# Output projection of a conv and attention layer: one accumulated sum with normalised inputs, or two sums with the norm's factor applied at eviction

## The reference

```
y_attn = rmsnorm(y_attn, g_attn_out) * silu(z_attn)      # 512 channels
y_conv = rmsnorm(y_conv, g_conv_out) * silu(z_conv)      # 512 channels
y = concatenate([y_attn, y_conv], axis=-1) @ w_out       # (512, 1024) @ (1024, 1024)
x = x + gate[:, None, :] * y
return rmsnorm(x, g_final)                               # mean of squares per token, eps 1e-6
```

## Time and profile before

| | us |
|---|---|
| median of 3 runs (lowest, highest) | 285.13 (285.1, 285.28) |
| the profiled execution, its own time | 284.59 |
| its span in the profile | 282.8 |
| TensorE busy | 268.6 (95%) |
| VectorE busy | 197.0 (70%) |
| ScalarE busy | 141.1 (50%) |
| GpSimd busy | 115.0 (41%) |

### The profile page before, as it was taken

How to read it: one execution, slowest core, us unless ns; L and a number is a source line. 1 busy time by engine, 2 the same in 40 slices (tenths; PEclk the granted TensorE clock), 3 DMA queues, 4 the chain that set the end, 5 groups by cost and what they waited for, 6 DMA issues and landing times.

```text
span 282.8 us, 3727 instructions
## 1 busy us (share of the span) xinstructions
PE 268.6 (95%) x1292; PEld 222.1 (79%) x1292; DVE 197.0 (70%) x351; ACT 141.1 (50%) x237; POOL 115.0 (41%) x73
## 2 busy tenths in 40 slices
PE   5889999899999999999999999999999999999990
PEld 1567888688888888888888888888888878888880
DVE  4898888799989976889899865922773531305564
ACT  4845355367059733673633364637196583402331
POOL 2500001466433433191363322343356999922410
PEclk9999999999999999999999999999999999999998
DMA  5999944296702462067334102332503444500113
GB/s 204 381 417 419 406 186 129 72 418 203 255 3 74 122 194 96 0 233 288 112 82 141 52 27 74 111 72 96 206 14 137 153 145 167 206 0 2 75 74 149
DMA packets 12405, 43.82 MB, mean 155 GB/s; under 512 B 2145, under 2 KB 2145, under 8 KB 10978
## 3 DMA queue, kind: packets, MB, share of 16 engines
q1 hardware_dynamic: 12242, 43.32, 43.0%
q10 hardware_dynamic: 144, 0.26, 0.2%
HBM read 38.33 MB, written 2.10 MB: 143 GB/s over the span
## 4 chain that ended last, share of the span: by engine, by line
PE 74%; ACT 6%; issue 6%; POOL 4%; DVE 4%; DMA 3%; SPq 1%; POOLq 0%; ACTq 0%; DVEq 0%
PE ps L1009 17%; PE ps L1011 17%; PE ps L1010 17%; PE ps L1068 4%; POOL w_lo L579 3%; PE ps L1153 3%; PE ps L1083 2%; PE ps L1145 2%; DMA xt<-in_x 2%; PE ps L1089 2%; DVE mod_junk L688 2%; PE ps L1081 1%; PE ps L1087 1%; PE ps L1128 1%; PE ps L1127 1%
## 5 line engine op out<-in xcount | busy, mean ns | idle before, releaser
L579 POOL TENSOR_TENSOR w_lo<-raw,w_hi 128x1024 fp32r<-128x1024 f32 x29 | 74.1, 2559 | 123.8 <-ACT w_hi L327 123.7
L1009 PE MATMUL ps<-h_lo,w_hi 128*128 128x512 f32 x200 | 78.9, 395 | 0.0
L1011 PE MATMUL ps<-h_hi,w_hi 128*128 128x512 f32 x200 | 78.0, 390 | 0.0
L1010 PE MATMUL ps<-h_hi,w_lo 128*128 128x512 f32 x200 | 77.9, 389 | 0.0
L1011 PEld LDWEIGHTS ps<-h_hi,w_hi 128*128 128x128 f32 x200 | 37.6, 188 | 8.0
L1010 PEld LDWEIGHTS ps<-h_hi,w_lo 128*128 128x128 f32 x200 | 37.6, 188 | 7.2
L1009 PEld LDWEIGHTS ps<-h_lo,w_hi 128*128 128x128 f32 x200 | 37.6, 188 | 7.1
L688 DVE CUSTOM_DVE_ANT_0 mod_junk<-ada,c_bc 128x1024 f32<-128x1024 f32 x22 | 34.1, 1549 | 1.1
L327 ACT ACTIVATE w_hi<-raw 128x1024 fp32r<-128x1024 f32 x29 | 30.4, 1051 | 6.9 <-DMA raw<-in_wslots 6.9
L394 ACT ACTIVATE probs<-probs,rmin 128x384 f32<-128x384 f32 (+3 forms) x32 | 17.6, 552 | 30.0 <-DVE rmin L814 30.0
L824 DVE TENSOR_SCALAR probs<-probs,prec 128x384 f32<-128x384 f32 (+3 forms) x32 | 21.4, 733 | 0.3
(11 more groups left out here) (153 smaller groups left out, 503.3 us busy)
## 6 DMA issues: line engine op xcount, KB each, us to landing
raw<-in_wslots SPq DMA_DIRECT2D x33, 512.0 KB, 3.4
ada<-in_ada SPq DMA_DIRECT2D x11, 1024.0 KB, 8.9
raw<-in_whead SPq DMA_DIRECT2D x8, 448.0 KB, 7.2
xt<-in_x SPq DMA_DIRECT2D x4, 512.0 KB, 4.9
x<-in_x SPq DMA_DIRECT2D x4, 512.0 KB, 5.8
out<-x SPq DMA_DIRECT2D x3, 512.0 KB, 2.7
ada<-in_ada SPq DMA_DIRECT2D x2, 512.0 KB, 8.0
qs<-q_lo SPq DMA_DIRECT2D x16, 64.0 KB, 2.0
```

Source lines behind the costliest of these rows:

```text
L579: nc.gpsimd.tensor_tensor(lo, src[:, :], hi.bitcast(F32), ALU.subtract).then_inc(s_lo, 1)
L1009: nc.tensor.matmul(o, a_hi, b_lo, start=start, stop=False)
L1010: nc.tensor.matmul(o, a_lo, b_hi, start=False, stop=False)
L1011: return nc.tensor.matmul(o, a_hi, b_hi, start=False, stop=stop)
```

## The change

The factor is a number per token, and the projection's output has tokens on partitions. So y goes into the projection without it, and it is applied to the output. Since the halves have different factors, they can't share a sum.

- `y_diag`, `y_rows` and `y_scaled` are gone, for both halves.
- The conv half has a list of its own, `CONV`: pieces 0 to 6 and one of 512 columns in place of pieces 7 and 8. Both halves open and close their own sums in the same banks; the attention share of a piece starts once the conv share has been read (`om_ok`).
- VectorE evicts 17 times in place of 9, each with one scalar_tensor_tensor (bank × factor × gate) and the addition to x2: eight for conv, then nine for attention.
- The split of y no longer waits for the norm. `y_high(0, 0)` to `(0, 2)` and `y_low(0, 0)` to `(0, 2)` move up among the weight slots; for the attention half `y_high(1, ·)` waits for `attn_gated` and stands, as before, behind slot 32.
- `y_sums(1)` on VectorE moves from behind `join_halves(3, 1)` to behind the eviction of conv piece 1. `y_rstd(1)` stays where it is on GpSimd, between slots 29 and 30.

```
+    CONV = PIECES[:7] + [(3, 512, 1024, 3)]
+    NC = len(CONV)
...
-            def y_diag(g):
-                act.wait_ge(rs_ok, g + 1)
-                for m in range(TT):
-                    ins = nc.scalar.activation(diag[:, m, :], ident[:, :], ACT.Copy, scale=rsy[:, g, m:m + 1])
-                ins.then_inc(diag_ok, 1)
+            def y_high(g, p):
+                if g == 0:
+                    act.wait_ge(yc_gated, p + 1)
+                    act.wait_ge(mod_step, 2 * NADA)
+                else:
+                    act.wait_ge(ya_gated, p + 1)
+                    act.wait_ge(pv_out, 2 * NP)
+                nc.scalar.activation(group(g)[1][:, p], group(g)[0][:, p], ACT.Copy).then_inc(y_hi, 1)
...
-            def y_scaled(g, p):
-                dve.wait_ge(bc_out, g + 1)
-                dve.wait_ge((yc_gated, ya_gated)[g], p + 1)
-                y = group(g)[0][:, p]
-                nc.vector.tensor_tensor(y, y, bank((4, 3)[g]), ALU.mult).then_inc(y_norm, 1)
...
             join_halves(3, 1)
-            y_sums(1)
             attn_gated(3)
-            for p in range(NP):
-                y_scaled(1, p)
...
+            def residual(g, e):
+                m, lo, hi, b = (CONV, PIECES)[g][e]
+                i = NC * g + e
+                dve.wait_ge(acc_out[g], e + 1)
+                if i == 0:
+                    dve.wait_ge(gate_ok, 2)
+                if g == 0 and e % 2 == 0:
+                    dve.wait_ge(x2_in[m], 16)
                 if e == 0:
+                    dve.wait_ge(rs_ok, g + 1)
+                if i >= 2:
+                    dve.wait_ge(x2_ok, i - 1)
+                o = om[:, i % 2, 0:hi - lo]
+                nc.vector.scalar_tensor_tensor(out=o, in0=bank(b, 0, hi - lo), scalar=rsy[:, g, m:m + 1],
+                                               in1=gate[:, lo:hi], op0=ALU.mult, op1=ALU.mult).then_inc(om_ok, 1)
+                dve.wait_ge(om_ok, i + 1)
...
                 nc.vector.tensor_tensor(x2[:, m, lo:hi], x2[:, m, lo:hi], o, ALU.add).then_inc(x2_ok, 1)
+
+            for e in range(NC):
+                residual(0, e)
+                if e == 1:
+                    y_sums(1)
...
-            pe.wait_ge(y_norm, NP)
+            pe.wait_ge(ssq_ok, 1)
             project(0, 3)
-            y_rows(1)
...
             project(0, 6)
+            pe.wait_ge(ssq_ok, 2)
+            project(0, 7)
+            pe.wait_ge(om_ok, 2)
             for p in range(NP):
...
+                project(1, 0, [p])
+                project(1, 1, [p])
+            for e in range(2, len(PIECES)):
+                pe.wait_ge(om_ok, e + 1)
+                project(1, e)
```

More of the change, by code:

```diff
@@ L188, in build @@
         sq_add = [sem("sqc_add"), sem("sqa_add")]
[L189 to L191 removed]
+        ssq_out, ssq_ok, rs_ok = sem("ssq_out"), sem("ssq_ok"), sem("rs_ok")
+        y_hi, y_lo = sem("y_hi"), sem("y_lo")
         gcol_ok, gdiag_ok, gate_bc, gate_ok = sem("gcol_ok"), sem("gdiag_ok"), sem("gate_bc"), sem("gate_ok")
[L193 removed]
+        acc_out, om_ok, x2_ok, x2_sq, x2_g = [sem("acc_conv"), sem("acc_attn")], sem("om_ok"), sem("x2_ok"), sem("x2_sq"), sem("x2_g")
         last_sq, x2_left = sem("last_sq"), sem("x2_left")
@@ L496, in _ @@
             slot(20)
+            y_high(0, 0)
             other_half(2, 1)
@@ L500, in _ @@
             slot(21)
+            y_high(0, 1)
             exponents(3, 0)
@@ L505, in _ @@
             slot(23)
+            y_high(0, 2)
             square_y(0, 3)
@@ L517, in _ @@
             probs_high(3, 1)
-            y_high(0)
+            y_high(0, 3)
             silu("ZA3")
@@ L523, in _ @@
             slot(W_ATTN0 + 1)
-            y_diag(1)
             slot(W_ATTN0 + 2)
             slot(W_ATTN0 + 3)
-            y_high(1)
+            for p in range(NP):
+                y_high(1, p)
             def square_out(e):
                 m, lo, hi, _ = PIECES[e]
-                act.wait_ge(x2_ok, e + 1)
+                act.wait_ge(x2_ok, NC + e + 1)
                 if e:
@@ L589, in y_rstd, with y_low @@
                 nc.gpsimd.tensor_tensor(rsy[:, g, :], ssy[:, g, :], nhalf[:, 0:TT], ALU.pow).then_inc(rs_ok, 1)
[L591 to L596, removed]
+            def y_low(g, p):
+                pool.wait_ge(y_hi, NP * g + p + 1)
+                raw_y, hi, lo = group(g)
+                nc.gpsimd.tensor_tensor(lo[:, p], raw_y[:, p], hi[:, p].bitcast(F32), ALU.subtract).then_inc(y_lo, 1)
             for n in range(12):
@@ L612, in _ @@
             add_square(1, 2)
-            for n in range(21, 24):
-                slot(n)
+            y_low(0, 0)
+            slot(21)
+            y_low(0, 1)
+            slot(22)
+            slot(23)
+            y_low(0, 2)
             add_square(0, 3)
@@ L621, in _ @@
             slot(28)
-            y_low(0)
+            y_low(0, 3)
             add_square(1, 3)
@@ L627, in _ @@
                 slot(n)
-            y_low(1)
+            for p in range(NP):
+                y_low(1, p)
             for m in range(TT):
@@ L940, in _ @@
             attn_gated(2)
-            for p in range(NP):
-                y_scaled(0, p)
             join_halves(3, 0)
@@ L945, in _ @@
             join_halves(3, 1)
-            y_sums(1)
             attn_gated(3)
-            for p in range(NP):
-                y_scaled(1, p)
-            def residual(e):
-                m, lo, hi, b = PIECES[e]
-                dve.wait_ge(acc_out, e + 1)
-                if e == 0:
[L956 to L961, removed]
-                nc.vector.tensor_tensor(o, bank(b, 0, hi - lo), gate[:, lo:hi], ALU.mult).then_inc(om_ok, 1)
-                dve.wait_ge(om_ok, e + 1)
+            def residual(g, e):
[6 more added lines that the diff above has]
+                    dve.wait_ge(x2_in[m], 16)
+                if e == 0:
+                    dve.wait_ge(rs_ok, g + 1)
[5 more added lines that the diff above has]
+                dve.wait_ge(om_ok, i + 1)
+                if i >= NC:
+                    dve.wait_ge(x2_ok, NC)
                 nc.vector.tensor_tensor(x2[:, m, lo:hi], x2[:, m, lo:hi], o, ALU.add).then_inc(x2_ok, 1)
+            for e in range(NC):
+                residual(0, e)
+                if e == 1:
+                    y_sums(1)
             def sum_out(m):
@@ L1177, in y_squares @@
                 ins.then_inc(ssq_out, 1)
-            def y_rows(g):
-                b = (4, 3)[g]
-                pe.wait_ge(diag_ok, g + 1)
-                for m in range(TT):
-                    ins = nc.tensor.matmul(bank(b, m * P, (m + 1) * P), ones[:, :], diag[:, m, :], start=True, stop=True)
-                ins.then_inc(bc_out, 1)
             def project(g, e, pairs=range(4)):
-                m, lo, hi, b = PIECES[e]
+                m, lo, hi, b = (CONV, PIECES)[g][e]
                 t = slice(m * P, (m + 1) * P)
@@ L1195, in project @@
                     ins = mm3(bank(b, 0, hi - lo), y_h[:, p, t], y_l[:, p, t], w_h[:, lo:hi], w_l[:, lo:hi],
-                              g == 0 and p == 0, g == 1 and p == NP - 1)
-                return ins
+                              p == 0, p == NP - 1)
+                if NP - 1 in pairs:
+                    ins.then_inc(acc_out[g], 1)
             unit("H0")
@@ L1245, in _ @@
             unit("ZA2")
-            y_rows(0)
             values(3, 0)
```

21 lines of the change are left out of this document (2 added, 19 removed).

## The result

| | before | after | ratio |
|---|---|---|---|
| first four runs of each | 285.20 us (285.1 to 285.44) | 290.33 us (287.88 to 291.95) | 1.0172 [1.011, 1.0233] |
| again, later (9 and 5 runs) | 285.24 us (284.45 to 286.15) | 289.63 us (288.36 to 291.43) | 1.0162 [1.0126, 1.0198] |

Slower, as forecast, but 2.8 us above the 287.5 that I gave and outside my range. The profiled execution took 290.19, span 288.4, against 284.59 and 282.8: +5.60.

What follows compares the result with a forecast made beforehand. TensorE, busy for 95% of the span, was taken as the bound. −1.62 − 0.53 + 1.55 + 2.9 + 0.15 = +2.45 us, giving 287.5 on the scale of the medians (285.13 before); range 284.9 to 288.7.

Steps and rivals of the forecast that it cites:

- two `y_rows`, old stall gone: TensorE loses two y_rows of 0.81 us each (−1.62) and the 0.53 us stall of values(3, 1) on pt_lo.
- wait ahead of `y_squares(0)`: TensorE waits for GpSimd's sum of squares, add_square(0, 3), delayed behind y_low(0, 2): 1.55 us lost.
- x2 in place (first eviction's start): First x2 load, issued at 236.3, lands 4.6 us later at 240.9; VectorE's first eviction waits for it.
- power on ssy(1): GpSimd's power waits for y_sums(1), behind x2's landing and two evictions on VectorE: starts at 243.95.
- slots 30–32 to first `y_low`'s end: GpSimd's slots and first attention y_low run from 244.95 to 255.0, including 1.6 us for collisions with VectorE's additions.
- TensorE ready for attention: TensorE comes to attention piece 0 at 252.85, against 250.64 in the kernel before.
- its wait: TensorE waits at attention piece 0 until the first y_low ends at 255.0: 2.2 us.
- second and third `y_low`: These come 1.70 us apart against 1.36 for six matmuls, so TensorE waits 0.34 us for each.
- tail: Three evictions in the ending chain become scalar_tensor_tensor from PSUM, a wide one 0.75 us against 0.69: +0.15 us.
- TensorE's clock: Nothing counted over the whole kernel, as the page grants 9 tenths or more in every slice but the last.
- rival 1: VectorE's plain addition is not held beside GpSimd's subtractions, which keep their pace: +0.1, 285.2 us; chance 0.12.
- rival 3: VectorE's new eviction from PSUM is held beside GpSimd as well: about +1.0, 288.5 us; chance 0.14.

Runs made afterwards that it cites:

- both_28: both, with ScalarE's copy of slot 28 moved behind other_half(3, 0) and probs_high(3, 1): 283.30 us, 0.9931 of the kernel before.
- both: The changed kernel with y_sums(1) back behind join_halves(3, 1) and add_square(0, 3) ahead of y_low(0, 2): 284.33 us, 0.9963 of the kernel before.
- warm_first: The changed kernel with three unused matmuls filling only TensorE's wait ahead of y_squares(0): 289.69 us, 1.0135 of the kernel before.
- add_first: The changed kernel with add_square(0, 3) ahead of y_low(0, 2) on GpSimd: 288.39 us, 1.0119 of the kernel before.

## Why the prediction was wrong

| step | forecast | measured |
|---|---|---|
| two `y_rows`, old stall gone | −1.62, −0.53 | no wait at `values(3, 1)`; `both_28` −2.0 with the tail |
| wait ahead of `y_squares(0)` | 1.55 | 1.45 |
| x2 in place (first eviction's start) | 240.9 | 241.98 |
| power on ssy(1) | 243.95 | 245.00 |
| slots 30–32 to first `y_low`'s end | 10.05 | 9.86 |
| TensorE ready for attention | 252.85 | 253.21 |
| its wait | 2.2 | 2.79 |
| second and third `y_low` | 0.68 | 0.77 (22.85 less the 22.08 of `both`) |
| tail | +0.15 | +0.17 (7.31 less 7.14) |
| TensorE's clock | 0 | 2.24 in the profile, 1.8–2.1 in the median |

**Right:** direction, both new waits with their releasers, the chain from x2's landing to the late `y_low`, that the plain addition is held (rival 1 false), that the eviction from PSUM is not (rival 3 false), and 0.75 for it. Without the clock the rows give −2.15 + 1.45 + 2.79 + 0.77 + 0.17 = +3.0 where the forecast has +2.45. The difference is nearly all in one term, the wait of 2.2 that came out at 2.79. x2 was in place 1.1 later than I took it: the load was issued 0.3 later and took 5.2 us to land in place of 4.6. TensorE came 0.36 later too, and the first slot lost 0.15 to its collision and not 0.3; the price of a full collision, 0.43, was right. With both waits filled the kernel has 1.0098 [1.0075, 1.0122]; the forecast is 1.0083. The rows leave 5.60 − 3.03 − 2.24 = 0.33. The start-up put the profile 0.67 late, so some 0.3 of it was won back elsewhere; where is not traced. That 1.0098 and 1.0083 agree so well is in part luck, since the wait alone was 0.6 us too short in the sum.

**The step that failed** is the sentence "I count nothing for the clock: the page grants 9 tenths or more in every slice but the last". It takes the clock of a kernel whose TensorE hardly waits once its units run as that of one where I had just put two waits in, of 1.55 and 2.2 us. What the runs showed in its place is a clock at half for 6.8 us from within the second wait on, 6.1 of them under matmuls: 2.24 us in the profile, 1.8 to 2.1 in the median, most of the 2.8 by which the forecast missed. The trace of before held a case of either kind. In its head TensorE waits 1.35 us, and the clock stays at 1.00 from 9 to 12 us:

```profile
10.53 1.11 PE L1030 MATMUL ps<-ident,sin_k 128*128 128x128 f32 x4 [1.35 <-ACT cos_k L334]
```

At its end the clock does fall, 4.7 us after the last matmul. So the rows of before left open what a new wait between these two would do; they were no ground for nothing. The honest treatment was a term bounded from both sides: nothing, or every matmul behind the wait at double its pitch for some microseconds. With the 6.1 us of matmuls at half in the profile after, that is up to 3 us. The range ended at 288.7 for want of that term. The Trainium skill (TensorE: Matmul & The Clock Gate, HAM oscillation — how this bites in real kernels) says that a wait can throttle the array so that the work behind it starts at the lower clock, and its section What's actually happening that the moment at which the clock rises to full speed differs from run to run. The trace agrees on the first, in one of the two profiles above; what differs between our runs is more than the moment, it is whether the clock falls at all. I had not weighed it, and it was a rival of its own.

## What to carry to other kernels

A forecast that puts a new wait of a microsecond or more on TensorE must carry a term for the clock, and where a kernel's runs spread more than before, sort them by their mean clock first. To tell the price of the wait from that of the clock, fill the wait with matmuls that nobody reads: the wait stays, and the time that this saves is the clock's part. When a step is moved up or down a list written by hand, look at what it stands behind on every engine: here one reduction of 4 columns behind two evictions, and one addition behind one split, turned 2 us of gain into more than 4 of loss.

## What was not expected of the hardware

- The same wait of 2.8 us dropped the clock in one profile and not in another; behind it TensorE ran at half for 6.1 us of work before the clock came back. In the same profile a wait of 2.16 us in the head (9.1 to 11.3) left it at 1.00. With waits of 3.8 and 3.4 us (`warm_first`, `add_first`) it fell at 258.0, 0.5 and 1.5 us after TensorE had gone back to work. At the end of the kernel before it held longer: the last matmul ends at 275.66, and the first two of these stretches of its profile still have 1.00.

```profile
276.00:278.00 2.00, 0.00 (x0) 0.00 (x0) 1.82 (x7) 0.32 (x1) 0.00 (x0) 1.00 0.44 176
278.00:280.00 2.00, 0.00 (x0) 0.00 (x0) 0.89 (x2) 0.72 (x1) 0.54 (x1) 1.00 0.23 90
280.00:282.80 2.80, 0.00 (x0) 0.00 (x0) 0.00 (x0) 0.00 (x0) 0.00 (x0) 0.56 0.50 187
```

- An addition of one column (0.16 us alone) lasts up to 1.94 beside a GpSimd subtraction, and costs GpSimd nothing that the rows show: the slots stay at 2.38. It is the full-size addition that holds GpSimd in turn, 0.41 to 0.44 each.
- scalar_tensor_tensor from PSUM with two SBUF operands (factor and gate) lasts 0.74 to 0.75, at full GpSimd work too.
